# One transformer layer pair in float32 on one core: the weight split on POOL as four instructions of 256 columns instead of one of 1024

## The reference

```python
x = x + 0.5 * swiglu(rms_norm(x), ffn1_w_in, ffn1_w_out)
x = x + hybrid_mixer(rms_norm(x), ...)          # conv + SSD scan, and differential attention
x = x + memory_cross_attention(rms_norm(x), rms_norm(mem), w_cq, w_ck, w_cv, w_co)
x = x + 0.5 * swiglu(rms_norm(x), ffn2_w_in, ffn2_w_out)
x = rms_norm(x)
# second block: stick-breaking attention beside a gated convolution, an MLP, a gated projection
x = x + rms_norm(mixed @ w_o);  x = x + rms_norm(square(relu(h @ w_up)) @ w_down)
x = x + sigmoid(rms_norm(x) @ w_ple_gate) * (p @ w_ple_proj)
```

## Time and profile before

| what | value |
|---|---|
| median of 3 runs | 2289.01 us (2285.53 to 2289.84) |
| the profiled execution | 2285.15 us, span 2283.3 us |
| PE busy | 2174.2 us (95%) |
| DVE busy | 905.3 us (40%) |
| ACT busy | 774.2 us (34%) |
| POOL busy | 910.3 us (40%) |
| granted TensorE clock, mean | 0.989 |

### The profile page before, as it was taken

One profiled execution on the slowest core, in us unless ns is written; L12 is line 12 of the kernel. 1 busy time (PEld: TensorE's weight loads), 2 busy tenths in 40 slices (PEclk: granted clock), 3 DMA queues, 4 the chain that ended last, 5 costly groups with the idle time before them and its releaser, 6 DMA issues.

```text
span 2283.3 us, 27733 instructions
## 1 busy us (share of the span) xinstructions
PE 2174.2 (95%) x9940; PEld 1767.6 (77%) x9940; DVE 905.3 (40%) x1469; ACT 774.2 (34%) x1170; POOL 910.3 (40%) x384
## 2 busy tenths in 40 slices
PE   7999999999988989898999999999999979999988
PEld 6888888778876657776888888887677868888876
DVE  4222212855822656124322222208763467013126
ACT  4222222234414434423332323325544333223223
POOL 4444443443142112732444444443333445444444
PEclk9999999999999999999999999999999999999999
DMA  6233332222122112421233333322222313333331
GB/s 218 93 100 96 101 105 87 89 83 68 52 88 75 56 33 82 151 82 38 92 101 93 99 101 99 99 96 68 65 74 65 104 53 102 104 99 101 94 109 46
DMA packets 58906, 203.41 MB, mean 89 GB/s; under 512 B 6296, under 2 KB 7704, under 8 KB 58824
## 3 DMA queue, kind: packets, MB, share of 16 engines
q1 hardware_dynamic: 53568, 192.96, 27.0%
q10 hardware_dynamic: 5256, 9.30, 1.2%
HBM read 200.12 MB, written 4.74 MB: 90 GB/s over the span
## 4 chain that ended last, share of the span: by engine, by line
PE 52%; issue 30%; POOL 12%; DVE 5%; ACT 1%; POOLq 0%; DVEq 0%; ACTq 0%
PE bank L421 16%; PE bank L423 16%; PE bank L422 16%; POOL w_lo L387 12%; DVE stick_sum L1814 1%; DVE pn_t L1870 1%; DVE gx_lo L1383 1%; PE bank L781 1%; DVE x L1872 1%; PE bank L842 1%; PE bank L483 0%; PE bank L485 0%; PE bank L484 0%; PE bank L840 0%; DVE stick_sum L1809 0%
## 5 line engine op out<-in xcount | busy, mean ns | idle before, releaser
L387 POOL TENSOR_TENSOR w_lo<-w_raw,w_hi 128x1024 fp32r<-128x1024 f32 x364 | 885.1, 2434 | 1322.5 <-ACT w_hi L951 1322.0
L421 PE MATMUL bank<-gx_hi,w_hi 128*128 128x512 f32 x1696 | 671.0, 396 | 44.6 <-DVE gx_lo L1383 13.5
L423 PE MATMUL bank<-gx_hi,w_lo 128*128 128x512 f32 x1696 | 663.4, 391 | 0.0
L422 PE MATMUL bank<-gx_lo,w_hi 128*128 128x512 f32 x1696 | 663.3, 391 | 0.0
L951 ACT CAST w_hi<-w_raw 128x1024 fp32r<-128x1024 f32 x364 | 378.9, 1045 | 394.5 <-PE bank L423 353.4
L421 PEld LDWEIGHTS bank<-gx_hi,w_hi 128*128 128x128 f32 x1696 | 320.4, 189 | 123.6 <-issue 41.2
L423 PEld LDWEIGHTS bank<-gx_hi,w_lo 128*128 128x128 f32 x1696 | 320.2, 189 | 67.9
L422 PEld LDWEIGHTS bank<-gx_lo,w_hi 128*128 128x128 f32 x1696 | 320.8, 189 | 64.9
L421 PE MATMUL bank<-ff_hi,w_hi 128*128 128x512 f32 x352 | 136.9, 389 | 0.0
L422 PE MATMUL bank<-ff_lo,w_hi 128*128 128x512 f32 x352 | 136.9, 389 | 0.0
L423 PE MATMUL bank<-ff_hi,w_lo 128*128 128x512 f32 x352 | 136.9, 389 | 0.0
(11 more groups left out here) (324 smaller groups left out, 2766.4 us busy)
## 6 DMA issues: line engine op xcount, KB each, us to landing
w_raw<-wstream SPq DMA_DIRECT2D x364, 512.0 KB, 3.5
bias_spread<-bias_rows ACTq DMA_DIRECT2D x1, 2560.0 KB
x<-xT ACTq DMA_DIRECT2D x2, 1024.0 KB, 10.3
outT<-ple_o SPq DMA_DIRECT2D x8, 256.0 KB, 2.0
square<-bias_spread ACTq DMA_DIRECT2D x4, 256.0 KB, 2.7
rfin_row<-bias_spread ACTq DMA_DIRECT2D x4, 256.0 KB, 2.6
m_T<-memT ACTq DMA_DIRECT2D x1, 1024.0 KB, 5.5
p_T<-pT ACTq DMA_DIRECT2D x1, 512.0 KB, 3.9
```

Source lines behind the costliest of these rows:

```text
L387: nc.gpsimd.tensor_tensor(w_lo[:, s, :], w_raw[:, s, :], w_hi[:, s, :].bitcast(F32), ALU.subtract).then_inc(unit_lo, 1)
L421: nc.tensor.matmul(dst, hi, rhs[0], start=first, stop=False)
L422: nc.tensor.matmul(dst, hi, rhs[1], start=False, stop=False)
L423: return nc.tensor.matmul(dst, lo, rhs[0], start=False, stop=last)
```

## The change

A split is issued as four tensor_tensor instructions, one for each quarter of the unit's columns. The wait before the first stays; only the last one counts unit_lo. Nothing else is touched.

```diff
             def split_unit(r, s):
                 pool.wait_ge(unit_hi, r * RING + (s + 1))
-                nc.gpsimd.tensor_tensor(w_lo[:, s, :], w_raw[:, s, :], w_hi[:, s, :].bitcast(F32),
-                                        ALU.subtract).then_inc(unit_lo, 1)
+                for q in range(4):
+                    part = slice(q * UNIT // 4, (q + 1) * UNIT // 4)
+                    ins = nc.gpsimd.tensor_tensor(w_lo[:, s, part], w_raw[:, s, part], w_hi[:, s, part].bitcast(F32),
+                                                  ALU.subtract)
+                ins.then_inc(unit_lo, 1)
```

## The result

The changed kernel takes 2269.72 us (median of four runs, 2268.64 to 2271.24) where the kernel before takes 2289.43 (2285.53 to 2291.32): a ratio of 0.9918, 95% interval 0.9906 to 0.9930, so 16 to 21.5 us won. The forecast was 2274.5 in a range of 2267 to 2292. The two profiled executions differ by less, 14.7 us (2285.15 and 2270.48): the one of before was faster than all four runs behind that median.

What follows compares the result with a forecast made beforehand. TensorE bounds the kernel (95% busy); POOL costs only where its splits stall VectorE instructions TensorE awaits. Gains 16.3 minus losses 1.8 give 14.5 us: 2270.7 against the profiled execution, 2274.5 as median; range 2267 to 2292.

Steps and rivals of the forecast that it cites:

- rival 2: Ports not handed to VectorE between pieces, so each stall is 3.04, not 2.38 us: +17.8, 2306.8 us; chance 0.10.
- The price of a piece: Each 256-column split: 0.22 us fixed plus 0.54, so 0.76 us; four take 3.04, 0.66 us more per unit.
- Rival 3: A piece's fixed cost is larger: at 1.05 us a piece, dense stretch and start lose; +13.4, 2302 us; chance 0.08.
- Convolution, 7.1 us: Convolution stage: shorter VectorE stalls let TensorE set the pace (5.5 us) and remove its idling for dt_T (1.6).
- Rival 1: Convolution waits add up beyond 1.2 us per tile, VectorE still sets the pace, 7.1 us not won: 2281.6; chance 0.12.
- Stick-breaking stage, 7.4 us: TensorE's four idle stretches for L1771: three close (5.0 us), the second shrinks by 2.35 us; 7.4 us won.
- Entry to the memory projections, 1.8 us: L1703 waits one piece instead of one split (1.5 us), plus 0.3 for sums in the same chain: 1.8 won.
- z_tok, nothing: Sixteen L1617 beside three splits: nearly every remaining one waits for one of 12 pieces; zero gain, within 1 us.
- The start, 1.5 us: First units: three of 3.04 us plus turns with sums and gx_lo delay unit 2; 1.5 us lost, 0.5 to 2.5.
- mix_attn, 0.3 us: Split from 884.48 takes 0.66 us more, making TensorE wait 0.2 to 0.3 us; counted as 0.3 lost.
- The densest stretch, nothing: Memory projections: 14 units need 42.6 us, 45.4 are there; nothing lost, limit 3.24 us a unit.
- Rival 4: Idle stretches close, but something just behind them holds TensorE as long: 2289, give or take 4; chance 0.12.

Runs made afterwards that it cites:

- second profile of before: The kernel before, unchanged, run and profiled once more: 2288.05 us (11 runs), ratio 1.0001; the profiled execution has 2289.08.
- the version with a whole head: Against the kernel before: first four units split whole, all others in four pieces; 2267.32 us against 2288.28, ratio 0.9903.

## Why the prediction was right, point by point

- **What bounds the kernel, and the exclusion.** Right. One POOL instruction at a time holds VectorE's two-input instructions off, and the next POOL instruction of the same unit lets one in. The trace after has it at the start: pieces and VectorE's instructions in turn, 1.13 us apart. So the rule of the Trainium skill ("SBUF — State Buffer", section "SBUF: two separate sides"), a lock kept for the whole instruction, agrees with the trace, 842 ns at most for L1817 where it was 2517. The other rule of the Trainium skill, that a core begins the next Pool instruction as soon as its share of the last is done ("GPSIMD Engine Reference", section 2.1), did not become a gap-free hold of the ports: rival 2 is out.
- **The price of a piece.** 0.76 us forecast. Twelve pieces take 8.44 us where VectorE is quiet, 0.70 each, so a unit is 2.8 and not 3.04 us:

```profile
917.11 8.44 POOL L389 TENSOR_TENSOR w_lo<-w_raw,w_hi 128x256 fp32r<-128x256 f32 x12 [3.69 <-ACT w_hi L954]
```

  The fixed part was drawn from L400, another operation, as 0.22 us. Pieces of 256 and the whole split (2.38) give (2.38 - 0.70) / 768 = 2.2 ns a column and 0.14 fixed, and the pieces of 128 follow: 33 in 13.94 us with a few turns of VectorE among them, 0.42 each. Rival 3 is out.
- **Convolution, 7.1 us.** 6.7 in the profile and 6.1 alone. VectorE's stall per tile fell from 1.9 to about 0.7 us (three L1512 of 1.00 us instead of 0.75), less than the 1.2 that it may have. Rival 1 is out for four pieces. With two pieces it is what happens (the last tiles 5.86 us apart), and the gain there is 4.5.
- **Stick-breaking stage, 7.4 us.** 9.5. The four stretches closed as forecast, but for 0.94 us. The working had 2.35 us for each chain and the rows give 2.75 (5.25 - 2.50). The idle stretches make 7.8 of the 9.5 us. The other 1.7 lie in conv2, and the trace shows most of them as TensorE's clock, a term the working does not have. In both profiles of before the first matmuls behind the stretch of 3.67 us start about 0.43 us apart:

```profile
1607.82 0.76 PE L421 MATMUL bank<-gx_hi,w_hi 128*128 128x512 f32 x1 [3.67 <-DVE cc_t L1771]
1608.39 0.63 PE L422 MATMUL bank<-gx_lo,w_hi 128*128 128x512 f32 x1
1608.81 0.63 PE L423 MATMUL bank<-gx_hi,w_lo 128*128 128x512 f32 x1
...
1611.19 0.40 PE L423 MATMUL bank<-gx_hi,w_lo 128*128 128x512 f32 x1
```

  The ninth starts 3.37 us after the first, and 1.92 in the changed kernel behind 0.94 us of idling: 1.45 us. (Behind the stretch of 2.14 us they start 0.23 us apart in the kernel before too.) The granted clock of conv2 is 0.98 before and 1.00 after; the variant with pieces only there has the same length to 0.01 us.
- **Entry to the memory projections, 1.8 us.** 6.1 in the profile, 4.2 alone. This is the term that was mis-sized. Two things failed in it. The stretch of 2.68 us was counted with one stall of L1703 (1.5 us), though L1373 before it stands behind a split as well, in the same chain (1.86 us instead of 0.69); the stretch went entirely. With the one behind m_lo that is 3.3 us less idling in the two stages. And TensorE's clock was taken as given: the granted clock of ck rose from 0.90 to 1.00, and the other 2.8 us are matmuls that follow each other faster, which no step had. Against the second profile of before the term is 5.2 us and not 6.1. The two L1373 were in the same view as the row that was quoted.
- **z_tok, nothing.** 10.67 us became 10.02: 0.65 us won, inside the 1 us. Sixteen instructions in turns with twelve pieces take about as long as behind three whole splits.
- **The start, 1.5 us.** 4.0. Mis-sized the other way. The sum had three units of 3.04 and two or three holds of 0.5 us. There are six VectorE instructions between 14 and 20 us, each of which takes a turn, and a piece that has waited for one takes 1.17 instead of 0.70. That gives the 2.2 us of idle time. The other 1.8 us is TensorE: its matmuls start 0.43 us apart until 25.9 us (until 20.0 in the kernel before), and 0.23 us apart from then on:

```profile
25.04 0.63 PE L425 MATMUL bank<-gx_lo,w_hi 128*128 128x512 f32 x1
25.46 0.63 PE L426 MATMUL bank<-gx_hi,w_lo 128*128 128x512 f32 x1
...
26.47 0.39 PE L426 MATMUL bank<-gx_hi,w_lo 128*128 128x512 f32 x1
26.70 0.39 PE L424 MATMUL bank<-gx_hi,w_hi 128*128 128x512 f32 x1
```

  The windows view shows a granted clock of 1.00 for all of it, so here the spacing tells what the clock row does not. The longer slow phase goes with the idle stretch; the version with a whole head has neither (0.43 us apart until 21.0).
- **mix_attn, 0.3 us.** 0.8 us of waiting for w_lo. The price of a wait was right in kind; again turns with VectorE (L1386 and L1706 beside the pieces) were left out of it.
- **The densest stretch, nothing.** Right, and the limit of 3.24 us a unit is borne out from the other side: with eight pieces (3.4 us a unit) cv becomes 3.9 us longer. By that limit it would have been 14 x 0.14 = 2.0 us; what the rest is was not followed.
- **The total.** 14.5 us by terms that were off by +4.6 (entry, with mix_attn in it), +2.1 (stick-breaking stage), -2.5 (start) and -0.4 (convolution), in sum +3.8: these places alone make 18.3 us. The median says 19.7 (16 to 21.5). The two profiled executions say 14.7, and that this is the forecast number is chance: the stretches k to mix_attn and qk2 to v2 took 1.8 + 1.6 us longer in the one of after, and the one of before took 4 us less than its kernel's median. Rival 4, something just behind the stretches that holds TensorE as long, is out by the time: no part of the interval reaches 1.

## What to carry to other kernels

Where POOL and VectorE both work from SBUF, expect the length of one POOL instruction as the longest wait of a VectorE instruction that reads two tensors from SBUF (with one, two, four and eight pieces L1814 lasted 2517, 1402, 842 and 567 ns at most, and 278 to 284 in the clear); look for VectorE instructions whose maximum is far above their median, and for what waits behind them on TensorE, before looking at either engine's busy share. Cut the POOL instruction only as far as the waits on the critical chain ask for, and only in those stages: each cut adds 0.14 us, and against a dense VectorE stream each piece also pays a turn of half a microsecond, which is dear exactly where somebody waits for POOL itself. Take the sum from several places with the whole chain in view, and take a second profile of the kernel before first; it tells which stages differ by themselves, though two profiles do not find them all. Where TensorE idles for some microseconds, count also the matmuls behind the stretch that start at the lower level: here that was 1.45 us in conv2 and up to 2.8 at the entry.

## What was not expected of the hardware

- A short POOL instruction between two long ones, behind a wait, gives VectorE one more turn: the third and the fourth mask pass around it, where the third had to sit out the second long split. 3.33 us for the four masks instead of 5.23.
- L1617, which reads one tensor from SBUF and a column of factors, is held up by POOL like the instructions with two tensors: 10.67 us for 16 before, 10.02 after, and 0.34 us for one in the clear.
- TensorE's slow phase at the start (matmuls 0.43 us apart) ended 5.9 us later where 2.2 us of idling interrupted it, and the granted clock of the windows view reads 1.00 throughout it.
- Two executions of the same kernel have their lower-clock stretches at different places (0.96 against 0.87 in 840 to 880 us, 0.96 against 0.91 in 1025 to 1065 us), and the stages around these two windows are 2.2 and 1.7 us longer in the second; its whole time is 3.9 us longer.
